# The head of a two-layer decoder kernel: all first loads on one DMA queue in order of need, memory transposes between the first weight pieces

## The reference

```python
for l in range(DEPTH):
    h = rms_norm(x, mix_norm[l])
    z = h @ w_in[l]
    ...
    x = x + merged @ w_out[l]
    x = x + memory_xattn(rms_norm(x, xa_norm[l]), rms_norm(mem, mem_norm[l]),
                         xa_wq[l], xa_wk[l], xa_wv[l], xa_q_norm[l], xa_k_norm[l], xa_wo[l])
    x = x + peer_ffn(...)
```

## Time and profile before

| what | value |
|---|---|
| median of three runs | 2128.26 us (2128.0 to 2128.49) |
| profiled execution, its own time | 2128.71 us |
| its span in the profile | 2126.9 us |
| PE busy | 2112.7 us, 99% of the span |
| POOL, DVE, ACT busy | 1706.3, 1255.2, 1194.2 us |
| bytes moved | 367.87 MB, 173 GB/s on average |

### The profile page before, as it was taken

The page is one execution under the profiler, slowest core; times in us unless marked ns, Lnnn a source line. Parts: engine busy times, 40 slices in busy tenths (PEclk is TensorE's granted clock), DMA queues, the critical chain, the costliest instruction groups (busy, mean ns, idle before and its releaser), DMA issues.

```text
span 2126.9 us, 48181 instructions
## 1 busy us (share of the span) xinstructions
PE 2112.7 (99%) x14342; PEld 1818.0 (85%) x14342; DVE 1255.2 (59%) x2545; ACT 1194.2 (56%) x2291; POOL 1706.3 (80%) x1316
## 2 busy tenths in 40 slices
PE   9999999999999999999999999999999999999999
PEld 7888899999888888888888888999988888888887
DVE  5766459876666555433248664598766665553233
ACT  5556665565555545556555566655555555545565
POOL 7767678988888888888897676799888888888887
PEclk9999999999999999999999999999999999999999
DMA  8434445555545554555574344455545555555555
GB/s 287 159 124 134 149 147 176 183 178 177 168 158 167 169 171 164 191 200 189 191 255 147 127 141 138 150 182 183 184 165 167 167 167 167 168 169 198 190 192 179
DMA packets 101790, 367.87 MB, mean 173 GB/s; under 512 B 11600, under 2 KB 12880, under 8 KB 101456
## 3 DMA queue, kind: packets, MB, share of 16 engines
q1 hardware_dynamic: 97632, 354.46, 50.3%
q10 hardware_dynamic: 4080, 12.42, 1.6%
HBM read 365.78 MB, written 1.05 MB: 172 GB/s over the span
## 4 chain that ended last, share of the span: by engine, by line
PE 96%; DVE 2%; ACT 1%; issue 1%; POOL 0%; ACTq 0%; POOLq 0%; DVEq 0%
PE acc L1268 17%; PE acc L1354 11%; PE acc L1356 11%; PE acc L1355 11%; PE acc L1267 7%; PE acc L1008 5%; PE acc L1010 5%; PE acc L1009 5%; PE aux L1312 4%; PE acc L1260 3%; PE acc L1258 3%; PE acc L1259 3%; PE aux L941 2%; PE acc L1271 1%; PE aux L1168 1%
## 5 line engine op out<-in xcount | busy, mean ns | idle before, releaser
L518 POOL TENSOR_TENSOR w_lo<-raw,w_hi 128x512 fp32r<-128x512 f32 x1312 | 1706.1, 1312 | 412.6 <-ACT w_hi L552 325.6
L552 ACT ACTIVATE w_hi<-raw 128x512 fp32r<-128x512 f32 x1348 | 843.8, 629 | 625.9 <-PE acc L1268 214.6
L1268 PE MATMUL acc<-h_rows,w_hi 128*128 128x512 f32 x1504 | 530.6, 397 | 0.0
L1354 PE MATMUL acc<-w_hi,eg 128*128 128x512 f32 x1020 | 401.0, 393 | 0.0
L1356 PE MATMUL acc<-w_hi,eg 128*128 128x512 f32 x1020 | 397.5, 390 | 0.0
L1355 PE MATMUL acc<-w_lo,eg 128*128 128x512 f32 x1020 | 397.0, 389 | 0.0
L2058 DVE TENSOR_TENSOR eg<-big,eg 128x256 fp32r<-128x256 f32 x256 | 149.7, 585 | 407.2 <-ACT eg L814 405.3
L1267 PE MATMUL acc<-h_rows,w_lo 128*128 128x256 f32 x1316 | 367.6, 279 | 0.0
L1268 PEld LDWEIGHTS acc<-h_rows,w_hi 128*128 128x128 f32 x1504 | 275.5, 188 | 50.8
L1267 PEld LDWEIGHTS acc<-h_rows,w_lo 128*128 128x128 f32 x1316 | 248.1, 189 | 8.4
L1356 PEld LDWEIGHTS acc<-w_hi,eg 128*128 128x128 f32 x1020 | 191.4, 188 | 40.6
(11 more groups left out here) (284 smaller groups left out, 2969.0 us busy)
## 6 DMA issues: line engine op xcount, KB each, us to landing
raw<-stream_dram SPq DMA_DIRECT2D x674, 512.0 KB, 3.3
big<-parb_dram ACTq DMA_DIRECT2D x2, 2128.0 KB, 10.0
big<-mem_dram ACTq DMA_DIRECT2D x2, 1024.0 KB, 5.4
big<-pm_dram ACTq DMA_DIRECT2D x2, 768.0 KB, 14.8
X<-x_dram ACTq DMA_DIRECT2D x1, 1024.0 KB, 9.5
out_dram<-X SPq DMA_DIRECT2D x4, 256.0 KB, 2.1
big<-parr_dram ACTq DMA_DIRECT2D x2, 448.0 KB, 12.0
big<-mem_dram ACTq DMA_DIRECT2D x1, 512.0 KB, 4.9
```

The lines of the kernel that those rows point to most:

```text
L518: nc.gpsimd.tensor_tensor(w_lo[:, k % SLOTS, :], raw[:, k // PER_CHUNK, k % PER_CHUNK, :], w_hi[:, k % SLOTS, :].bitcast(F32), ALU.subtrac ...
L552: nc.scalar.activation(w_hi[:, k % SLOTS, :], raw[:, (k // PER_CHUNK) % RAW, k % PER_CHUNK, :], ACT.Copy).then_inc(hi_ready, 1)
L1268: ins = pe_.matmul(acc[:, bank_of, :], w_hi[:, r % SLOTS, at], h_rows[:, kt, :, :], start=(kt == 0), stop=(kt == KD - 1))
L1354: pe_.matmul(dst, eg[:, q % 2, 0, ts], w_hi[:, slot, :], start=start, stop=False)
```

## The change

The memory now comes in four parts of 256 columns. SP issues all first loads without waiting, in this order: memory part 0, chunk 0, part 1, chunk 1, part 2, chunk 2, part 3, chunk 3, `X`, the constants. ACT issues only the identity and the gains. The idle products are six ahead of memory group 0 and three between group 0 and group 1. Memory groups 2 and 3 stand behind pieces 1 and 3. On ACT the memory's group 0 comes ahead of piece 0, and three pieces instead of one stand ahead of the first square of `X`; the two pieces that stood between parameter DMAs go. DVE's statistics of the memory move one place back.

```diff
-WARM = 12
+WARM = 6
...
             for r in range(RAW):
-                if r == 1:
-                    sp.wait_ge(mem_first, 32)
-                if r == 3:
-                    sp.wait_ge(sig["mem_in"].sem, 32)
-                    sp.wait_ge(const_in, 16)
+                cs = slice(r * 256, (r + 1) * 256)
+                part_in = mem_part[r] if r < 3 else sig["mem_in"].sem
+                sp.dma_start(memx[:, :, cs], mem_rows[:, :, cs]).then_inc(part_in, 16)
                 sp.dma_start(raw[:, r], stream[r:r + 1].rearrange("o p (k c) -> p (o k) c", c=COL)).then_inc(chunk_in[r], 16)
+            sp.dma_start(X[:], x.rearrange("(t p) d -> p t d", p=P)).then_inc(x_in, 16)
+            sp.dma_start(cst[:, K_ID + P:K_END], consts[:, K_ID + P:K_END]).then_inc(const_in, 16)
...
-            hi_piece(0, 16, 1)
-            first.wait_filled("mem_T0")
-            act.dma_start(X[:], x.rearrange("(t p) d -> p t d", p=P)).then_inc(x_in, 16)
-            memory_hi(first, 0)
+            act.wait_ge(col_in, 16)
+            memory_hi(first, 0)
+            hi_piece(0, 16, 1)
             hi_piece(1, 16, 2)
             memory_hi(first, 1)
...
                 for t in range(T):
-                    hi(1)
+                    hi(1 if layer or t else 3)
...
-                    if layer or name != "zgw":
+                    if layer:
                         hi(1)
...
-            for i in range(4):
-                memory_T(first, i, True)
-            forget(1, *filled)
-            pe_.wait_ge(const_in, 16)
+            memory_T(first, 0, True)
+            idle_products(WARM // 2)
+            memory_T(first, 1, True)
+            forget(1, *filled[0:2])
...
-                    take((8, 3)[n])
+                    if layer == 0 and n == 0:
+                        for i in (2, 3):
+                            take(2)
+                            memory_T(e, i, True)
+                            forget(1, filled[i])
+                        take(4)
+                        pe_.wait_ge(const_in, 16)
+                    else:
+                        take((8, 3)[n])
...
             memory_lo(first, 1)
+            memory_lo(first, 2)
             memory_stats(0)
-            memory_lo(first, 2)
+            memory_lo(first, 3)
             memory_stats(1)
-            memory_lo(first, 3)
```

More of the change, by code:

```diff
@@ L375, in trunk @@
         x_in = sem("x_in")
-        ident_in, mem_first = sem("ident_in"), sem("mem_first")
+        ident_in, col_in = sem("ident_in"), sem("col_in")
+        mem_part = [sem(f"mem_part{i}") for i in range(3)]
         const_in = sem("const_in")
@@ L473, in _ @@
         def _(sp):
+            mem_rows = mem.rearrange("(t p) d -> p t d", p=P)
             for r in range(RAW):
-                if r == 1:
-                    sp.wait_ge(mem_first, 32)
-                if r == 3:
-                    sp.wait_ge(sig["mem_in"].sem, 32)
-                    sp.wait_ge(const_in, 16)
+                cs = slice(r * 256, (r + 1) * 256)
+                part_in = mem_part[r] if r < 3 else sig["mem_in"].sem
+                sp.dma_start(memx[:, :, cs], mem_rows[:, :, cs]).then_inc(part_in, 16)
                 sp.dma_start(raw[:, r], stream[r:r + 1].rearrange("o p (k c) -> p (o k) c", c=COL)).then_inc(chunk_in[r], 16)
+            sp.dma_start(X[:], x.rearrange("(t p) d -> p t d", p=P)).then_inc(x_in, 16)
+            sp.dma_start(cst[:, K_ID + P:K_END], consts[:, K_ID + P:K_END]).then_inc(const_in, 16)
             with sp.Fori(0, DEPTH * CHUNKS // RAW - 1) as i:
@@ L538, in _ @@
             first = Engine(act, 0, act_step)
-            mem_rows = mem.rearrange("(t p) d -> p t d", p=P)
-            act.dma_start(memx[:, :, 0:COL], mem_rows[:, :, 0:COL]).then_inc(mem_first, 16)
             act.dma_start(ident, consts[:, K_ID:K_ID + P]).then_inc(ident_in, 16)
-            act.dma_start(col[:], cols[0:1].rearrange("o p c -> p (o c)")).then_inc(mem_first, 16)
-            for at in (COL, COL + 256):
-                act.dma_start(memx[:, :, at:at + 256], mem_rows[:, :, at:at + 256]).then_inc(sig["mem_in"].sem, 16)
-            act.dma_start(cst[:, K_ID + P:K_END], consts[:, K_ID + P:K_END]).then_inc(const_in, 16)
+            act.dma_start(col[:], cols[0:1].rearrange("o p c -> p (o c)")).then_inc(col_in, 16)
             def hi_piece(k, turn_value, free_value):
@@ L899, in _, with idle_products @@
             pe_.wait_ge(idle_rows, 1)
-            for _ in range(WARM):
-                pe_.matmul(acc[:, 3, 0:P], sel[:, 0:P], sel[:, P:2 * P], start=True, stop=True)
+            def idle_products(n):
+                for _ in range(n):
+                    pe_.matmul(acc[:, 3, 0:P], sel[:, 0:P], sel[:, P:2 * P], start=True, stop=True)
+            idle_products(WARM)
             pe_.wait_ge(ident_in, 16)
-            pe_.wait_ge(mem_first, 32)
             def memory_T(e, i, start=False):
-                if not start or i >= 2:
+                if start and i < 3:
+                    pe_.wait_ge(mem_part[i], 16)
+                else:
                     e.wait("mem_in")
@@ L1406, in _ @@
             dve.sem_inc(sig["layer_free"].sem, PRIMED["layer_free"])
+            dve.sem_inc(sig["mem_in"].sem, 16)
             def memory_lo(d, i):
@@ L1423, in memory_stats @@
             def memory_stats(t):
+                for part_in in mem_part:
+                    dve.wait_ge(part_in, 16)
                 first.wait("mem_in")
```

## The result

The changed kernel takes 2131.52 us (median of 20 runs, 2129.82 to 2133.24), the kernel before in the same series 2128.19 us (20 runs, 2126.63 to 2129.74): a ratio of 1.0016 (95%: 1.0010 to 1.0023), or 3.3 us more. By the bound of 0.2% that is still no change, but it lies outside the range, and the interval leaves out 1. The profiled execution took 2133.22 us, near the top of its runs, with a span of 2131.1 us; the one of before took 2128.71.

What follows compares the result with a forecast made beforehand. PE, busy 2112.7 of 2126.9 us, was taken to bound the kernel. -0.9 + 1.0 - 1.8 + 1.85 - 1.5 gave -1.35 us; one low stretch made it +0.15: median 2128.4 us, range 2126.4 to 2131.0.

Steps and rivals of the forecast that it cites:

- The table load: On ACT at the head: its 1.28 us load starts after memory group 0, at 4.8 us, and is no longer covered.
- The wait for `X`: PE's standstill ahead of piece 6, from ACT waiting for `X`, goes: -1.8 us.
- The stall ahead of piece 5: New PE stall, as ACT makes piece 5 only after the high part of group 3: +1.85 us.
- Groups 2 and 3: Eight memory transposes moved between PE's pieces, with their waits, cost 1.0 us.
- chunk 8 behind `parb`: Rival, chance 0.07: chunk 8 lands at 38.5 us and piece 16 is late, +3.2 us, 2131.6 us.
- I take one low stretch, of the length seen (1.5 us): PE's clock: one low stretch likeliest in the new order too, turning the sum from -1.35 to +0.15 us.
- one long one from before piece 0: Rival, chance 0.27: two low clock stretches or one long one, +1.65, at most some +3 us, 2129.9 us.
- The "Nothing" under "The rest": Closer parameter issues, the two pieces made later and DVE's later statistics of the memory cost nothing.
- So 0 to 0.1 us: Behind the mark (the transposes of `xn`): PE's wait for piece 18, whose chunk follows `parb`, costs 0 to 0.1 us.
- Piece 0 at 9.1 us: PE's first piece starts at 9.1 instead of 10.01 us, a gain of 0.9 us.
- rival without a low stretch: Chance 0.18: the clock never falls, -1.35 us, or -1.9 if a small wait at 47.43 goes too: 2126.9 us.
- -0.9 + 1.0 - 1.8 + 1.85 = +0.15 us: Sum of earlier piece 0, groups 2 and 3 between pieces, removed wait for `X`, and new stall ahead of piece 5.

Runs made afterwards that it cites:

- fill_gap: Changed kernel with six more idle products behind memory group 1, in PE's gap ahead of piece 0: 2129.21 us.
- warm12: Changed kernel with twelve idle products ahead of memory group 0 instead of six, the three behind it kept: 2131.28 us.
- dma_groups: dma_only_2 with PE's memory groups 2 and 3 placed behind pieces 1 and 3, as in the changed kernel: 2129.83 us.
- dma_group3_later: dma_only_2 with memory group 3 alone moved from ahead of piece 0 to behind piece 1: 2127.33 us.
- gap_t3_lead: Changed kernel with six more idle products behind group 1, group 3 right behind group 2, and ACT's pieces in their old places in layer 0: 2128.70 us.
- early_table: Changed kernel with a dummy activation ahead of ACT's first wait, to load the table while ACT is idle: 2131.40 us.
- dma_only_2: Kernel before with the new DMA queues and order alone, PE's wait for the constants behind piece 7: 2128.54 us.
- early_params: Changed kernel with four of layer 0's six parameter transfers issued ahead of the first square of `X`: 2130.81 us.

## Why the prediction was wrong

**Right.** The table load stood behind group 0 and was exposed (5.25 us, forecast 4.8). The wait for `X` went: it was issued at 4.76 us and landed 10.4 us later. The stall ahead of piece 5 was 1.65 us by its row (forecast 1.85). Groups 2 and 3 cost 0.57 and 0.50 us on PE (forecast 1.0). No fall of the clock followed the stall ahead of piece 5. No chunk 8 behind `parb`.

**The clock, the step that failed first.** "I take one low stretch, of the length seen (1.5 us)": there was one, but ahead of piece 0, 6 us and more long, and it cost 2.4 us on pieces 0 and 1 alone. The text set it against a low stretch of before, as if both kernels had one in every run. Before kept its clock in 133 of 148 runs; the profiled one was an exception. So the gain of 1.5 us was never in its median, and the loss is in the median of after in full: 1.5 to 2.2 us by three pairs of kernels. The sum had the clock at 0. The rival with "one long one from before piece 0" had the mechanism, with 2129.9 us as its time and "at most some +3 us". Of its two reasons the gap was the right one (fill_gap); the six products less were not (warm12).

**The "Nothing" under "The rest"**, and the sentence **"So 0 to 0.1 us" behind the mark**, failed next. The working followed one chunk behind `parb`, and found it in time. It didn't follow ACT: the squares were 4.8 us later, four parameter issues stood without a piece among them, and PE reached the mark 2.6 us after `parb`'s issue instead of 5.8. In the profile this made 2.33 us behind the mark. Part of that is this execution's: its six issues took 4.33 us together (before 2.73), and in fill_gap's, with the same order and 3.02 us of issues, only 0.4 us were lost there, in an execution 1 us below fill_gap's median.

**Piece 0 at 9.1 us** was 0.7 us too early: group 0 began at 4.08 instead of 3.8 and was handed to ACT at 5.25 instead of 4.8, and 0.25 us lay between POOL and PE.

**Small slips in the working.** The twelve idle products of before span 5.49 us in the row, not 5.3. Part 1 of the memory was there at 6.6 us, not 5.8, which cost nothing. The 0.3 us for the signal stands in no row. A piece ready at 40.5 instead of 37.5 us is 3.0 us late, not 3.2. In the rival without a low stretch 2126.9 us goes with -1.35; -1.9 would give 2126.4. The chances add up to 0.99. None of these moves the forecast by more than 0.3 us.

**The account.** The forecast's sum without the clock was -0.9 + 1.0 - 1.8 + 1.85 = +0.15 us, and the clock came to 0 in it. fill_gap shows the first part alone, as it kept the clock in all runs: +1.18 us, or 1.0 more than forecast. The gap with its clock is the other part, 1.5 to 2.2 us, where 0 was forecast. Together that is 2.7 to 3.4 us, against the 3.3 measured. dma_groups, which has the new queue and the groups between the pieces but neither the new order on ACT nor the shorter idle products, has nearly the same first part, +1.37 us. The queue is at most 0.3 us of it, which can't be told from nothing; so the groups between the pieces are the most likely seat, at 1.0 us (1.8 by the runs that kept the clock), but two such small differences are an indication and no proof. Of the 1.0 us that the sum lacked, 0.7 is the late piece 0 and some 0.4 is lost behind the mark, both by single profiles. What the runs leave open: what causes the loss behind the mark, the short lead or the long issues; and why dma_group3_later is 1.8 us faster than gap_t3_lead (group 2 ahead of piece 0, the early table load, ACT's first piece ahead of the memory, the idle products and DVE's order differ together).

The best kernel, dma_group3_later, takes the new DMA order and moves one group only: 2127.33 against 2128.23 us (0.9986 to 1.0004), not told from no change; its variant with late `tril` and `pm` is as good (-0.84).

## What to carry to other kernels

Before pricing a removed loss, look whether the median has it: the profiled execution is one draw, and its low clock may be in one run of ten. When idle products are taken away at a kernel's head, look at what PE does in the last microseconds ahead of the first real piece, not at their number; six products put right there gave back 2 us, six put ahead of the first transposes 0.5, which can't be told from nothing. And when a helper engine's work is put in another order, count how far it is ahead of the main engine at the next meeting point: a stall of 1.7 us removed ahead of that point won 0.1 us with one order of the helper's work and 1.6 with the other.

## What the runs showed of the hardware

- The Trainium skill (ScalarE: Activation LUTs, What ACT_TABLE_LOAD costs) gives about 1283 ns for the load and another 1380 ns of drain. The first agrees with 1.28 us here; the second doesn't show: the next activation starts at 6.54 us, right behind a load from 5.25. Nor does it show at the switch to the square root, where ACT's activation before ended at 26.05 us:

```profile
26.07 1.28 ACT L613 ACT_TABLE_LOAD   x1
27.37 0.21 ACT L613 ACTIVATE st<-st 128x4 f32<-128x4 f32 x1
```

- The same DMA issue instruction on ACT's queue took 0.45 us in fourteen of the twenty profiles and 1.04 to 1.35 us in six (`parb`), with ACT's pieces behind it held up. The long one can also be another of the six: 1.53 us for `parr` in early_table, 1.25 for `lnrow` in gap_t3_lead, 1.53 for `pm` in dma_groups. No run here shows what decides it.
- The length of a standstill alone did not decide whether the clock fell. In the profiled executions 3.52 us directly ahead of piece 0 (warm12) left it at 1.00, as did two gaps of 1.3 and 1.4 us with a group of transposes between (dma_only_2). In the changed kernel it fell 1.4 us into a standstill of 2.54 us, in early_table right behind 2.07 us, in early_params behind 1.82 us (ahead of memory group 1). And it differs between runs of one program: warm12 kept the clock in four of eleven, dma_only_2 in five of eleven, the changed kernel in three of twenty.
